# Two blocks of a transformer on one core: part of the first output projection's preparation moves from ACT and DVE to GpSimd

## The reference, cut to what matters

```python
h = rmsnorm(x, norm_mix_g[l]) * (1.0 + sc1) + sh1
proj = jnp.einsum('bsd,de->bse', h, w_in[l])
u_f, q, k, v = jnp.split(proj, split_cols, axis=-1)
...
y_f = fourier_mix(u_f, w_fourier[l], b_fourier[l])
y_a = windowed_gqa(q, k, v, rel_bias, sink[l])
mixed = jnp.einsum('bse,ed->bsd', jnp.concatenate([y_f, y_a], axis=-1), w_out[l])
x = x + g1 * mixed
h2 = rmsnorm(x, norm_ffn_g[l]) * (1.0 + sc2) + sh2
x = x + g2 * expert_choice_moe(h2, w_router[l], w_gate[l], w_up[l], w_down[l])
```

## Time and profile before

| what | value |
|---|---|
| median of 3 runs | 2002.72 us (2002.11 to 2005.15) |
| the profiled execution, its own time | 2002.89 us |
| its span in the profile | 2001.1 us |
| PE busy | 1942.4 us, 97% |
| DVE busy | 917.8 us, 46% |
| ACT busy | 720.4 us, 36% |
| POOL busy | 14.5 us, 1% |
| banded attention on PE | 120.7 to 172.6 us |
| first output projection on PE | 172.9 to 231.4 us |

### The profile page before, as it was taken

The page is one execution under the profiler, slowest core; times in us unless marked ns, Lnnn a source line. Parts: engine busy times, 40 slices in busy tenths (PEclk is TensorE's granted clock), DMA queues, the critical chain, the costliest instruction groups (busy, mean ns, idle before and its releaser), DMA issues.

```text
span 2001.1 us, 23834 instructions
## 1 busy us (share of the span) xinstructions
PE 1942.4 (97%) x9831; PEld 1333.5 (67%) x9831; DVE 917.8 (46%) x1487; ACT 720.4 (36%) x1193; POOL 14.5 (1%) x25
## 2 busy tenths in 40 slices
PE   6999999999999899999999999999999999999999
PEld 4756643333333267767788887877777778888787
DVE  4375412222111145464466665335556356666533
ACT  4365211111111141575333333235443643333323
POOL 1000000000000000000000000000000000000000
PEclk8999999999999999999999999999999999999999
DMA  9678479999999951400233332322212023332311
GB/s 324 144 278 227 186 299 427 427 428 428 427 427 428 426 152 34 146 1 22 64 105 105 84 106 85 105 85 64 85 64 64 22 64 103 87 105 85 106 64 42
DMA packets 168038, 346.43 MB, mean 173 GB/s; under 512 B 19643, under 2 KB 142267, under 8 KB 152443
## 3 DMA queue, kind: packets, MB, share of 16 engines
q1 hardware_dynamic: 165907, 340.85, 46.8%
q10 hardware_dynamic: 1224, 2.15, 0.9%
q0 software_dynamic: 800, 1.91, 0.4%
HBM read 340.70 MB, written 4.19 MB: 172 GB/s over the span
## 4 chain that ended last, share of the span: by engine, by line
PE 87%; DMA 7%; DVE 3%; ACT 2%; issue 1%; SPq 0%; DVEq 0%
PE bank L2158 22%; PE bank L1398 13%; PE bank L2175 12%; PE bank L1972 10%; PE bank L1991 4%; PE bank L1348 2%; PE bank L912 2%; PE bank L953 2%; DMA moe_high<-in_w_up 2%; DMA norm_area<-in_w_down 2%; PE bank L932 2%; DMA work<-in_w_up 2%; PE bank L1336 2%; DMA ring<-in_w_in 1%; PE bank L1941 1%; PE bank L2003 1%
## 5 line engine op out<-in xcount | busy, mean ns | idle before, releaser
L561 DVE TENSOR_TENSOR ring_low<-ring,w_high 128x2048 fp32r<-128x2048 f32 (+1 forms) x91 | 207.7, 2283 | 127.5 <-ACT w_high L551 127.4
L551 ACT ACTIVATE w_high<-ring 128x2048 fp32r<-128x2048 f32 x90 | 171.3, 1905 | 218.4 <-PE bank L2158 174.0
L2158 PE MATMUL bank<-h_high,ring_low 128*128 128x512 f32 x640 | 249.7, 390 | 0.0
L2158 PE MATMUL bank<-low_ff,w_high 128*128 128x512 f32 x608 | 238.3, 392 | 0.0
L2158 PE MATMUL bank<-h_high,w_high 128*128 128x512 f32 x608 | 236.5, 389 | 0.0
L2175 PE MATMUL bank<-ff_split,w_high 128*128 128x512 f32 x704 | 222.4, 396 | 1.6 <-DVE work L2879 1.6
L2175 PEld LDWEIGHTS bank<-ff_split,w_high 128*128 128x128 f32 x704 | 132.3, 188 | 35.8 <-DVE work L2879 2.4
L2175 PE MATMUL bank<-ff_split,ring_low 128*128 128x512 f32 x352 | 139.2, 396 | 0.0
L2158 PEld LDWEIGHTS bank<-h_high,ring_low 128*128 128x128 f32 x640 | 120.3, 188 | 26.5
L2158 PEld LDWEIGHTS bank<-h_high,w_high 128*128 128x128 f32 x608 | 114.1, 188 | 25.2
L2158 PEld LDWEIGHTS bank<-low_ff,w_high 128*128 128x128 f32 x608 | 114.1, 188 | 24.5
(11 more groups left out here) (462 smaller groups left out, 3377.0 us busy)
## 6 DMA issues: line engine op xcount, KB each, us to landing
ring<-in_ffn_w_up SPq DMA_DIRECT2D x88, 512.0 KB, 5.1
ring<-in_w_gate SPq DMA_DIRECT2D x16, 2048.0 KB, 22.4
ring<-in_w_down SPq DMA_DIRECT2D x12, 2048.0 KB, 26.6
ring<-in_ffn_w_down SPq DMA_DIRECT2D x22, 1024.0 KB, 4.9
ring<-in_w_ada SPq DMA_DIRECT2D x18, 1024.0 KB, 7.8
const<-in_w_gate SPq DMA_DIRECT2D x8, 2048.0 KB, 22.4
work<-in_w_up SPq DMA_DIRECT2D x8, 2048.0 KB, 22.3
ring<-in_w_up SPq DMA_DIRECT2D x8, 2048.0 KB, 22.9
```

What stands on the lines that cost most here:

```text
L551: act.activation(high_of(n, words), slab_view(g)[:, 0:words], ACT.Copy).then_inc(sem("split_high"), 1)
L561: dve.tensor_tensor(ring_low[:, slot_of(g), 0:words], slab_view(g)[:, 0:words], high_of(n, words).bitcast(F32), ALU.subtract).then_inc(sem ...
L2158: mm = pe.matmul(bank[n % 6][:, :], st[k], mv[k], start=(k == 0), stop=(k == len(st) - 1))
```

## The change

Seven result tiles (0 to 6) of the first output projection and two slabs of its weights (0 and 1) are rounded and subtracted on POOL. ACT and DVE keep result tile 7 and slabs 2 and 3. `OUT1_HIGH_AT`, `OUT1_LOW_AT` and `out1_half_act` go, so the attention loop of ACT and DVE has nothing of the projection in it. On POOL a slab goes in 4 pieces of 512 columns (`PIECES`), all four roundings and then all four subtractions; a result tile is one rounding, a wait for it, and one subtraction. The slabs of the third projection, that POOL rounded before, are now also subtracted there, in the same pieces, and DVE's four subtractions go.

POOL's list behind the router DMA is now: slab 0, results 0 to 3, slab 1, results 4 to 6, and then, as before behind `odin_done`, the third projection's slabs. PE waits for `pool_result` and `pool_slab` in place of `out_high`, `out_low`, `split_high` and `split_low` for these.

```diff
+        def high_ready(n):
+
+            if n in POOLED:
+                return sem("pool_slab"), PIECES * (2 * POOLED.index(n) + 1)
+            return sem("split_high"), n + 1 - sum(x < n for x in POOLED)
+
+        def low_ready(n):
+
+            if n in POOLED:
+                return sem("pool_slab"), PIECES * (2 * POOLED.index(n) + 2)
+            return sem("split_low"), n + 1 - sum(x < n for x in POOLED)
...
+        def result_pool(pool, n, ready, o, y):
+
+            pool.wait_ge(*ready)
+            pool.tensor_copy(o, y).then_inc(sem("pool_result"), 1)
+            pool.wait_ge(*result_high(n))
+            pool.tensor_tensor(h_high[:, n % DT, :], y, o.bitcast(F32), ALU.subtract).then_inc(sem("pool_result"), 1)
+
+        def split_pool(pool, n):
+
+            g = split_slabs[n]
+            loaded(pool, g)
+            if high_before[n] is not None:
+                pool.wait_ge(*high_before[n])
+            w = SLAB // PIECES
+            for x in range(PIECES):
+                pool.tensor_copy(high_of(n, SLAB)[:, w * x:w * x + w], slab_view(g)[:, w * x:w * x + w]).then_inc(sem("pool_slab"), 1)
+            for x in range(PIECES):
+                pool.wait_ge(sem("pool_slab"), 2 * PIECES * POOLED.index(n) + x + 1)
+                at = slice(w * x, w * x + w)
+                pool.tensor_tensor(ring_low[:, slot_of(g), at], slab_view(g)[:, at], high_of(n, SLAB)[:, at].bitcast(F32), ALU.subtract)\
+                    .then_inc(sem("pool_slab"), 1)
...
+        def out1_split_pool(pool, k):
+
+            ready = (sem("four_copied"), k + 1) if k < DT // 2 else WIN_A.out(TT * (k - DT // 2 + 1) - 1)
+            result_pool(pool, k, ready, y_high1[:, k, :], ymix[:, k, :])
...
             pool.dma_start(w_rt, t["w_router"][0].rearrange("(k p) e -> p k e", p=P)).then_inc(sem("router_loaded"), 16)
+            split_pool(pool, OUT1_SPLIT)
+            for k in range(DT // 2):
+                out1_split_pool(pool, k)
+            split_pool(pool, OUT1_SPLIT + 1)
+            for k in range(DT // 2, DT - 1):
+                out1_split_pool(pool, k)
 
             pool.wait_ge(sem("odin_done"), len(odin_tiles))
             for i in range(len(od_out)):
-                for part in range(2):
-                    out3_split_pool(pool, i, part)
+                split_pool(pool, OUT3_SPLIT + i)
...
                     if m == 0:
-                        pe.wait_ge(sem("out_high"), k + 1)
+                        pe.wait_ge(*(result_high(k) if k < DT - 1 else (sem("out_high"), 1)))
                     pe.matmul(bank[m % 4][:, :], w_hi[:, k, :], y_high1[:, k, :], start=(k == 0), stop=False)
                     if m == 0:
-                        pe.wait_ge(sem("out_low"), k + 1)
+                        pe.wait_ge(*(result_low(k) if k < DT - 1 else (sem("out_low"), 1)))
...
-            OUT1_HIGH_AT = {1: 0, 2: 1, 3: 2, 4: 3, 6: 4, 10: 5, 14: 6}
-
-            def out1_act(step):
-                if step in OUT1_HIGH_AT:
-                    out1_high_act(act, OUT1_HIGH_AT[step])
-                if step in (15, 16):
-                    out1_half_act(act, step - 15)
-
-            attention_act(act, WIN_A, out1_act)
+            attention_act(act, WIN_A)
             out1_high_act(act, DT - 1)
-            split_act(act, OUT1_SPLIT + 1)
             ada_rows(1)
...
-            OUT1_LOW_AT = {2: 0, 3: 1, 4: 2, 5: 3, 8: 4, 12: 5, 16: 6}
...
-            attention_dve(dve, mark, WIN_A, out1_dve)
+            attention_dve(dve, mark, WIN_A)
             out1_low_dve(dve, DT - 1)
-            split_dve(dve, OUT1_SPLIT)
             ada_rows_dve(1)
-            split_dve(dve, OUT1_SPLIT + 1)
             ada_columns(1)
...
             def out3_parts_dve(u):
-                if 2 <= u <= 5:
-                    out_split_dve(dve, OUT3_SPLIT, (u - 2) // 2, (u - 2) % 2)
```

More of the change, by code:

```diff
@@ L551, in split_act, with result_high, result_low @@
             act.activation(high_of(n, words), slab_view(g)[:, 0:words], ACT.Copy).then_inc(sem("split_high"), 1)
-        def highs(n):
-            return n + 1 - (len(od_out) if n > OUT3_SPLIT else 0)
+        def high_ready(n):
[6 more added lines that the diff above has]
+            return sem("split_low"), n + 1 - sum(x < n for x in POOLED)
+        def result_high(n):
+            return sem("pool_result"), 2 * POOL_RESULTS.index(n) + 1
+        def result_low(n):
+            return sem("pool_result"), 2 * POOL_RESULTS.index(n) + 2
+        def result_pool(pool, n, ready, o, y):
[16 more added lines that the diff above has]
+                    .then_inc(sem("pool_slab"), 1)
         def split_dve(dve, n):
             g = split_slabs[n]
-            dve.wait_ge(sem("split_high"), highs(n))
+            dve.wait_ge(*high_ready(n))
             words = shape_of[g][0]
@@ L570, in out_split_act @@
                .then_inc(sem("split_high") if part else sem("out_half"), 1)
[L572 to L577, removed]
         def out_split_dve(dve, base, i, part):
@@ L582, in out_split_dve @@
             at = slice(SLAB // 2 * part, SLAB // 2 * (part + 1))
[L583 to L586, removed]
+            if part:
+                dve.wait_ge(*high_ready(base + i))
             else:
@@ L592, in out_split_dve @@
                 o.then_inc(sem("split_low"), 1)
[L594 to L603, removed]
+        def out1_split_pool(pool, k):
+            ready = (sem("four_copied"), k + 1) if k < DT // 2 else WIN_A.out(TT * (k - DT // 2 + 1) - 1)
+            result_pool(pool, k, ready, y_high1[:, k, :], ymix[:, k, :])
         def out1_high_act(act, k):
[L607 to L610, removed]
+            act.wait_ge(*WIN_A.out(TT * (k - DT // 2 + 1) - 1))
             act.activation(y_high1[:, k, :], ymix[:, k, :], ACT.Copy).then_inc(sem("out_high"), 1)
         def out1_low_dve(dve, k):
-            dve.wait_ge(sem("out_high"), k + 1)
+            dve.wait_ge(sem("out_high"), k - (DT - OUT1_ACT) + 1)
             dve.tensor_tensor(h_high[:, k, :], ymix[:, k, :], y_high1[:, k, :].bitcast(F32), ALU.subtract).then_inc(sem("out_low"), 1)
@@ L761, in build @@
         UP_SPLIT[1], DOWN_SPLIT[1] = split(ffn_w[1][0], third=2), split(ffn_w[1][1])
+        PIECES = 4
+        POOL_RESULTS = []
+        POOL_RESULTS += range(DT - 1)
+        OUT1_ACT = 1
+        OUT2_ACT = DT
+        POOLED = []
+        POOLED += [OUT1_SPLIT, OUT1_SPLIT + 1]
+        POOLED += [OUT3_SPLIT, OUT3_SPLIT + 1]
         def half(v, i, n=HD):
@@ L2131, in sub_norm @@
                             mm.then_inc(sem("sub_summed"), 1)
-            pe.wait_ge(sem("out_low"), DT + 4)
+            pe.wait_ge(sem("out_low"), OUT1_ACT + 4)
             start_pe(pe, [0, 1, 2, 3], out2_tiles, 12, sub_norm)
-            project_pe(pe, "out2", [0, 1, 2, 3], out2_tiles, started=12, ready=lambda k: (sem("out_low"), DT + k // 3 + 1),
+            project_pe(pe, "out2", [0, 1, 2, 3], out2_tiles, started=12, ready=lambda k: (sem("out_low"), OUT1_ACT + k // 3 - (DT - OUT2_ACT) + 1),
                        within=lambda: wide_sum(pe, "evpost", range(4, 7)),
@@ L2220, in _ @@
             attention_pe(pe, DIL_A, before_last=out3_begun)
-            pe.wait_ge(sem("out_low"), 2 * DT + 3)
+            pe.wait_ge(sem("out_low"), OUT1_ACT + OUT2_ACT + 3)
             start_pe(pe, [0, 1, 2, 3], out3_tiles, 9, begun=4)
-            project_pe(pe, "out3", [0, 1, 2, 3], out3_tiles, started=9, ready=lambda k: (sem("out_low"), 2 * DT + 4), within=lambda: wide_sum(pe, "odpost", range(4, 7)),
+            project_pe(pe, "out3", [0, 1, 2, 3], out3_tiles, started=9, ready=lambda k: (sem("out_low"), OUT1_ACT + OUT2_ACT + 4), within=lambda: wide_sum(pe, "odpost", range(4, 7)),
                        after=lambda i: wide_sum(pe, "odpost", range(4)) if i == 4 else None)
```

21 lines of the change are left out of this document (9 added, 12 removed).

## The result

The changed kernel takes 2017.97 us (median of 4 executions, 2016.75 to 2018.79), the kernel before beside it 2003.45 us: a ratio of 1.0070, 95% interval 1.0058 to 1.0082, or +14.5 us. The profiled execution took 2018.1 us with a span of 2016.3 us, against 2001.1 before. The forecast was 2016, slower.

The account below looks back on a forecast made before the run. Time is won or lost only where PE, 97% busy, waits; in the first projection it would wait for POOL. 11.3 + 1.7 + 0.5 = +13.5 us on 2002.7 gives 2016.2, so 2016; range 2006 to 2025.

Parts of the forecast that it names:

- What POOL must do: First output projection: POOL starts at 159.8 behind slab 0's load; 15 roundings at 0.57, 15 subtractions at 1.04, total 24.9 us.
- What leaves ACT: Seam after banded attention: roundings leaving ACT and subtractions leaving DVE win 1 to 2 us, if nothing else ends later.
- POOL disturbed by DVE: After 159.8, beside the last attention units: POOL loses 0 to 4.4 us to DVE's operations, 2.5 taken.
- DVE disturbed by POOL, the attention stretched: Last banded attention units: DVE waits for POOL, stretching them 3 to 5 us, end 176 or 178, hidden behind POOL.
- What PE sees: First output projection: PE starts the low product of k=6 at 187.3 in place of 176.0, +11.3 us.
- The clock: After PE's idle stretch in the first projection: granted clock falls, half speed costs 1.7 us (0 to 3.4).
- Given back later: After the first projection, up to the experts: the loads move with PE, so nothing is made up, 0.
- Third projection: At the dilated attention: POOL's added subtractions hold DVE up, from -1 to +2 us, +0.5 taken.
- A: Rival at the seam: POOL's work fits by 176.0, 0.52 us each, 1 to 2 us won, 2001; chance 0.08.
- B: Rival on POOL's subtraction: cheap at 0.57 us, POOL done at 179.1, kernel 2006 to 2008; chance 0.10.
- C: Rival on POOL's work: subtraction of 1.50 us or heavy interference, 2026 to 2028; chance 0.18 including what lies between.
- D: Rival at the first projection: PE's clock doesn't fall, 2014 to 2015; inside the forecast's own range, which has chance 0.62.

Follow-up runs that it names:

- e8_cast0: Kernel before, with only slab 0's rounding on POOL in 4 pieces of 512 columns, third projection as in the change: ratio 0.9992, -3.1 us.
- e11_cast16: Kernel before, with only slab 0's rounding on POOL in 16 pieces of 128 columns, third projection as in the change: ratio 0.9989, -2.1 us.
- e6_idle: Kernel before, plus 15 copies and 15 subtractions on POOL from slab 0's landing, outputs read by nobody: ratio 1.0031, +6.1 us.
- e1_order: Changed kernel with POOL's list reordered to results 0 to 5, slab 0, result 6, slab 1: ratio 1.0034, +7.4 us over the kernel before.
- e9_small: Changed kernel with only the two slabs, no results, on POOL, in 16 pieces of 128 columns, third projection too: ratio 1.0012, +1.9 us over before.
- e10_both: Changed kernel, POOL's list reordered by readiness and its first-projection operations cut to 128 columns: ratio 1.0008, +2.5 us over the kernel before.
- e7_busy: Changed kernel with idle matmuls on PE in its waits for results 4 to 6: ratio 1.0052, +10.3 us over the kernel before.
- e4_third: Kernel before with only the third projection's part of the change, its two slabs also subtracted on POOL: ratio 0.9996, -1.4 us.

## Why the prediction was right, step by step

**What POOL must do.** The start at 159.8 was 159.98. The wait at the head of the list was the first of two causes, as written. A rounding measured 0.57 in the slabs and 0.61 in the results, for 0.57. A subtraction measured 1.24 to 1.27 us for 1.04: this is the term that was sized wrong, by 15 x 0.2 = 3 us. A second input costs more than a second pass: between 128 and 512 columns the rounding grows by 0.33 us (3.85 / 16 = 0.24 to 0.57) and the subtraction by 0.83 (6.64 / 16 = 0.42 to 1.24), 2.5 times as much. The estimate from the Trainium skill ("GPSIMD Engine Reference", section "Performance versus the Vector engine") was 1.2 us; here the trace agrees with it and not with my model. The sign of being wrong, a subtraction over 1.3 us, was touched where DVE worked beside it: 1.36 on the mean in slab 1 (5.42 / 4), 1.39 in result 1.

**What leaves ACT.** "1 to 2 us" behind PE's last full unit: e8_cast0 and e11_cast16, where of the seam's work only the two half-slab roundings leave ACT, gain 1.0 us at the second output tile.

**POOL disturbed by DVE.** With the measured prices, from start to start, the list takes 2 x 7.15 (1546.03 to 1553.18) + 7 x 1.91 (183.14 to 185.05) = 27.7 us undisturbed, for the 24.9 of the prediction. It took 28.9 (159.98 to 188.92): 1.2 us lost, for the 2.5 taken. So the list was sized 2.8 us too short and the disturbance 1.3 too large. That the second error takes back half of the first is luck; 187.2 became 188.9.

**DVE disturbed by POOL, the attention stretched.** Predicted 176 to 178 for its end, measured 178.2. Predicted as hidden behind POOL: true in the changed kernel, where the chain never touches DVE. But the sentence leaves out how large it is alone: 6 us by the medians in e6_idle and 7 in e1_order (8.2 and 8.6 at the second output tile, of 15.2), half of the whole loss, since a stretched attention also goes with a lower clock (0.50 from 172 to 176, after PE had been busy 2.34 and 1.97 us in the two windows of 4 us before). As the change stands the two causes lie side by side, each hiding part of the other; 7.4 (e1_order) is not a remainder of 14.5 minus a separate 7. The rule that I named for it (the Trainium skill, "SBUF — State Buffer", section "Who interferes with whom": GpSimd and certain DVE operations lock each other out) agrees with the trace in what it touches: operations between SBUF tiles yes, the one that reads a bank and one SBUF input no. By the same section of the Trainium skill the one that comes second waits until the other's instruction is finished; the 3.68, 3.69 and 6.16 us of e9_small and e10_both are longer than that, and the measurement decides.

**What PE sees.** +11.3 predicted, +13.0 measured, by the price above.

**The clock.** 1.7 predicted, 2.24 read from the trace, 1.9 undone by e7_busy.

**Given back later.** 0 predicted; the shift is 15.20 after the first tile and 15.25 at the experts: right.

**Third projection.** +0.5 predicted; e4_third shows between -2.4 and +1.0 (its interval times 2004), so the sign wasn't to be had. In the changed kernel's profile nothing is added there.

**The sum.** 13.0 + 2.2 = 15.2, and 0 behind it: the profiled span is 15.2 longer, the medians 14.5; 13.5 was predicted (11.3 + 1.7 + 0.5). Term by term, 11.3 was 13.0, 1.7 was 2.2 and 0.5 was nothing that shows: the mechanism held. Of the rivals, A needs 0.52 us an operation (measured 0.6 and 1.25 and more), B a subtraction under 0.7, C one of 1.5, D a clock that stays. None holds.

## What to carry to other kernels

An idle engine isn't a free one. Its list is in order, so work that is ready must not stand behind a wait for a transfer: sorting POOL's list by readiness took back half of the loss without changing any work, though it moved some of it beside other units, which it then stretched by 2.3 us. And work on GpSimd is paid a second time where VectorE has short SBUF-to-SBUF operations on the critical chain: keep long GpSimd operations out of that stretch, and don't trust small pieces to let VectorE in.

## What the runs showed of the hardware that I had not expected

- A DVE operation can sit out not one POOL operation but a whole run of them: 3.68 and 3.69 us in e9_small and 6.16 us in e10_both, for operations of 0.16 and 0.17 us, with POOL in pieces of 0.42 us. Each ended with POOL's run of subtractions. In the changed kernel, with pieces of 512, the longest hold-up of a small one that I saw in the last units was 1.20 us (L1121). It isn't a matter of the stage: in the first projection of e9_small DVE's 128x2 operations got in within 0.5 us beside slab 0's pieces, and the one of 128x8 was shut out for 3.68 us beside slab 1's. What decides is open.
- POOL is held as well, and both lose: in e6_idle 2.56 for 0.6 us and 3.24 for 2.29 us at the same time.
- Which DVE operations were held: TENSOR_SCALAR, TENSOR_TENSOR, SCALAR_TENSOR_TENSOR and COPY between SBUF tiles, down to 128x2. Not held: RECIPROCAL on 128x2 (153 ns, 161 before) and the operation on a bank with one SBUF input.
